# Ten unused TensorE products ahead of the first normed block of each half, at three norms of a decoder step

## What is computed

```python
def rmsnorm(x, g):
    xf = x.astype(F32)
    y = xf * lax.rsqrt(jnp.mean(xf * xf, axis=-1, keepdims=True) + EPS)
    return y.astype(x.dtype) * g
...
        x = x + rmsnorm(o, p['norm_mix_post'][l])
        f, cp = conv_ffn(rmsnorm(x, p['norm_ffn_pre'][l]), p['w_up'][l], p['conv_w'][l],
                         p['conv_b'][l], p['w_down'][l], conv_prev[l])
        new_conv.append(cp)
        x = x + rmsnorm(f, p['norm_ffn_post'][l])
```

## Time and profile before

| | before |
|---|---|
| median of 3 runs | 1521.39 us |
| lowest, highest | 1520.93, 1525.54 us |
| span of the profiled execution, first to last instruction | 1519.0 us |
| what the median has over that span | 2.4 us |
| PE busy, share of the span | 1413.4 us, 93% |
| PEld / DVE / ACT / POOL busy | 86% / 64% / 38% / 42% |
| mean granted TensorE clock | 0.971 of full speed |

### The profile page before, as it was taken

One profiled execution on the slowest core, in us unless ns is written; L12 is line 12 of the kernel. 1 busy time (PEld: TensorE's weight loads), 2 busy tenths in 40 slices (PEclk: granted clock), 3 DMA queues, 4 the chain that ended last, 5 costly groups with the idle time before them and its releaser, 6 DMA issues.

```text
span 1519.0 us, 32537 instructions
## 1 busy us (share of the span) xinstructions
PE 1413.4 (93%) x12097; PEld 1313.9 (86%) x12097; DVE 976.7 (64%) x1658; ACT 576.7 (38%) x1019; POOL 638.5 (42%) x420
## 2 busy tenths in 40 slices
PE   6986978989999999999799989999989999999997
PEld 6984758979999999999699966657889999999997
DVE  5769967576773167765748688753677761376755
ACT  4544354344432133422415235432454431234323
POOL 1586422304444334433177888402223443344430
PEclk9998789989999999999999999999999999999999
DMA  5344364213333232332145769995213233233321
GB/s 173 114 117 79 63 169 123 83 44 85 99 94 98 77 97 83 102 98 75 45 121 164 226 175 308 331 340 157 69 57 97 84 103 90 83 91 88 104 83 62
DMA packets 289082, 180.47 MB, mean 119 GB/s; under 512 B 54248, under 2 KB 274572, under 8 KB 288924
## 3 DMA queue, kind: packets, MB, share of 16 engines
q1 hardware_dynamic: 288412, 179.07, 40.9%
q10 hardware_dynamic: 576, 0.13, 0.0%
HBM read 167.10 MB, written 10.63 MB: 117 GB/s over the span
## 4 chain that ended last, share of the span: by engine, by line
PE 70%; DVE 14%; issue 8%; ACT 2%; SPq 2%; DMA 1%; POOL 1%; DVEq 0%; ACTq 0%; POOLq 0%
PE big L2649 58%; PE big L2715 3%; PE misc L2800 2%; DVE tmp L1261 2%; PE big L2746 2%; DVE y L1738 1%; DVE rstd L1219 1%; DVE x L1744 1%; DVE w_lo L1208 1%; DVE x_lo L1251 1%; SPq L597 1%; PE misc L2770 1%; ACT yc L2506 1%; DVE cp L1261 1%; ACT w_hi L2144 1%
## 5 line engine op out<-in xcount | busy, mean ns | idle before, releaser
L949 POOL TENSOR_TENSOR w_lo<-raw,w_hi 128x1024 fp32r<-128x1024 f32 (+2 forms) x153 | 393.8, 2574 | 708.9 <-ACT w_hi L2144 548.4
L2144 ACT ACTIVATE w_hi<-raw 128x1024 fp32r<-128x1024 f32 (+2 forms) x179 | 198.5, 1109 | 582.1 <-PE big L2649 539.0
L2649 PE MATMUL big<-x_hi,w_hi 128*128 128x264 f32 x1984 | 406.7, 287 | 8.4 <-DVE uc L1827 2.8
L2649 PE MATMUL big<-x_hi,w_lo 128*128 128x264 f32 x1984 | 400.8, 283 | 0.0
L2649 PE MATMUL big<-x_lo,w_hi 128*128 128x264 f32 x1984 | 398.8, 283 | 0.0
L2649 PEld LDWEIGHTS big<-x_hi,w_hi 128*128 128x128 f32 x1984 | 305.9, 189 | 13.1 <-issue 4.7
L2649 PEld LDWEIGHTS big<-x_lo,w_hi 128*128 128x128 f32 x1984 | 305.6, 189 | 0.0
L2649 PEld LDWEIGHTS big<-x_hi,w_lo 128*128 128x128 f32 x1984 | 305.3, 189 | 0.0
L1831 DVE SCALAR_TENSOR_TENSOR yc<-uc,convw,yc 128x512 f32<-128x512 f32 x88 | 136.7, 1554 | 113.2 <-ACT yc L2506 113.2
L2649 PE MATMUL big<-h_hi,w_hi 128*128 128x264 f32 x616 | 125.1, 284 | 6.3 <-DVE h_lo L1846 6.3
L2649 PE MATMUL big<-h_hi,w_lo 128*128 128x264 f32 x616 | 123.9, 282 | 0.0
(11 more groups left out here) (434 smaller groups left out, 2330.8 us busy)
## 6 DMA issues: line engine op xcount, KB each, us to landing
raw<-in_w_up SPq DMA_DIRECT2D x88, 512.0 KB, 3.9
raw<-in_w_down SPq DMA_DIRECT2D x32, 704.0 KB, 4.7
areas<-in_cache_k SPq DMA_DIRECT2D x41, 384.0 KB, 4.5
areas<-in_cache_v SPq DMA_DIRECT2D x41, 384.0 KB, 4.7
raw<-in_w_in SPq DMA_DIRECT2D x16, 512.0 KB, 4.2
raw<-in_w_out SPq DMA_DIRECT2D x16, 512.0 KB, 4.2
raw<-in_w_kv SPq DMA_DIRECT2D x12, 512.0 KB, 4.6
spare<-in_cache_k SPq DMA_DIRECT2D x12, 384.0 KB, 4.5
```

Of the source, the lines that this page charges most:

```text
L949: pool.tensor_tensor(w_lo[slot][:, 0:kb, :], raw[slot][:, 0:kb, :], w_hi[slot][:, 0:kb, :].bitcast(F32), ALU.subtract).then_inc(lo_made, 1)
L2144: A.activation(w_hi[slot][:, 0:kb, :], raw[slot][:, 0:kb, :], ACT.Copy).then_inc(hi_made, 1)
L2649: ins = pe.matmul(big[2 * slot + b_][:, 0:c1 - c0], w[slot][:, k, :], r[:, c0:c1], start=(k == 0 and n_ == 0), stop=(k == kb - 1 and n_ == 2))
```

## The change

Ten products that nothing reads are added twice at each of the three norms. `spin(o, 5)` issues five pairs of 128-column products of `meanw` (as weights) and `ident` (as the moving operand) into PSUM bank o; the real product that follows starts its bank anew and overwrites it. The first ten stand ahead of block k = 0 of half 0 in panel 0, the second ten ahead of block k = 0 of half 1 in panel 0. In half 0 the wait for the PSUM bank moves ahead of the spin, and the wait for w_lo stays behind it.

```diff
+SPUN = (5, 5)
...
+            def spin(o, count):
+
+                for _ in range(count):
+                    for c in range(2):
+                        pe.matmul(o[:, P * c:P * c + P], meanw[:], ident[:], start=True, stop=True)
+
             def first_pair(base, name, before):
 
                 add = x_stats(name)
@@
                         q = base + p_
                         slot = q % 2
                         if b_ == 0:
+                            pe.wait_ge(panel_read, q - 1)
+                            if p_ == 0:
+                                spin(big[2 * slot], SPUN[0])
                             pe.wait_ge(lo_made, q + 1)
-                            pe.wait_ge(panel_read, q - 1)
                         for k in range(KD):
                             if p_ == 0:
+                                if b_ and k == 0:
+                                    spin(big[2 * slot + 1], SPUN[1])
                                 x_split(KD * b_ + k)
```

## The result

Over 13 runs each, the changed kernel took 1531.13 us in the median (1523.25 to 1533.23) and the kernel before 1525.76 us (1520.76 to 1530.24): ratio 1.0035, 95% interval 1.002 to 1.005. That is 5.4 us slower, 3 to 8 by the interval. The sign and the place were as predicted, and the size was close (7.1 us forecast, 1.0047). The kernel before itself spreads over 9.5 us from run to run. The three runs that the prediction started from, which are among the 13, had their median 4.4 us low, and its profiled execution (span 1519.0) was one of the two fastest. Two executions of the kernel before beside the experiments took 7594 and 4704 us, and the ratios leave them out.

What follows compares the result with a forecast made beforehand. PE was taken to set the pace from panel 1 on, DVE at each norm's start. First ten 0, second ten 3 x 2.36 = 7.1 us, clock 0: 1521.4 + 7.1 = 1528.5 us, range 1522.0 to 1532.5.

Steps and rivals of the forecast that it cites:

- The first ten are hidden: Start of half 0, panel 0: ten products take 2.4 us while PE waits for DVE, so they cost 0.
- They save nothing: First gap of each norm: filling it should keep the clock up, but DVE sets the pace there; gain nothing.
- rival 2: At the norms: low-clock stretches thought covered by DVE cost too, all five go, 11.9 us saved, 1516.6 us; chance 0.05.
- The second ten cost in full: Ahead of half 1, panel 0, where PE has no cover: 2.4 us at each norm, 3 x 2.36 = 7.1 us.
- The clock at nothing, kept for the range: Low-clock stretches at the norms may come or go, 1.7 us each, no sign; mean 0, used for the range.
- Rival 1: Through the norms the clock stays at 2.4 GHz, three costly stretches go, 6.1 us saved against 7.1, 1522.4 us; chance 0.13.
- Rival 3: Layer 1 attention: page loads absorb the 4.7 us of f0 and x1, only f1's 2.4 remain, 1523.8 us; chance 0.07.
- Rival 4: Added products: a record costs 0.23 us without load overlap, three times ten 13.8 us, 1535.3 us or more; chance 0.07.

Runs made afterwards that it cites:

- e2: The changed kernel with only the first ten products at each norm, none in the second place; ratio 0.9995 to the kernel before.
- e6: The changed kernel with twenty products in the first place and none in the second; ratio 1.0012 to the kernel before.
- e7: The changed kernel with ten products in the first place, ten ahead of the second w_lo wait, none before half 1; ratio 1.0000 to the kernel before.
- e1: The changed kernel without its products, only the PSUM bank wait moved; ratio 1.0001 to the kernel before.
- e11: The changed kernel without its products, as e1, profiled once more; 1527.45 us.
- e3: The changed kernel with only the second ten products at each norm; ratio 1.0039 to the kernel before, 6.0 us slower.
- e5: The changed kernel with no first products and twenty in the second place; ratio 1.0091 to the kernel before, 13.9 us slower.
- e8: e4 plus six products (f0, f1) or ten (x1) behind the last block of the norm; ratio 0.9982 to the kernel before.
- e9: e8 plus ten products in the first place and eight ahead of block 6 of half 0; ratio 0.9978 to the kernel before.
- e4: The changed kernel with its products replaced by ten at each norm ahead of the second w_lo wait (panel 1, half 0); ratio 0.9986 to the kernel before.

## Why the prediction came out as it did

**The first ten are hidden: right.** The prediction had them stick out 0.4 us at f0, under the wait of block 1. They took 2.2 us and not 2.4, and block 0 was not late at all: it starts 2.02 us behind the end of `last_pair` in both kernels. e2 gave 0.9995.

**They save nothing: right in the sum, half right in the reason.** The prediction said that the low stretches at 314 and 1096 lie under DVE, and they do: ACT took up the post-norm's second root at the same point of its order with the clock up, 8.46 us behind the end of `last_pair` against 8.45 before:

```profile
320.40 0.41 ACT L2481 ACTIVATE y<-x 128x264 f32<-128x264 f32 x1
320.71 0.45 ACT L2178 ACTIVATE sd<-misc,eps 128x256 f32<-128x256 f32 x1
```

That disposes of rival 2. What it missed: in half 0 the pace is DVE's, block 6 starts 12.0 to 12.2 us behind `last_pair` at f0 and f1 in all thirteen profiles, whatever the clock does, and a clock that stays up only leaves idle time ahead of it. The kernel before's trace had this wait too, at x1, where the clock had been up, and the prediction counted only the one behind it (PE in order of time):

```profile
735.39 0.39 PE L2746 MATMUL big<-x_hi,w_hi 128*128 128x264 f32 x1 [2.09 <-DVE x_lo L1251]
```

The clock then fell at a later wait. In all twelve norms with the first gap filled and the one at block 6 open (after, e2, e6, e7) it fell within 6 us of block 6's start, in ten of them within 1.2 us: in the changed kernel at 324.7, 741.1 and 1109.7, with block 6 at 324.27, 735.16 and 1108.61. In the fifteen norms with neither the first gap nor the second filled (before, e1, e11, e3, e5) it fell within 6 us there in nine, and not at f1 of the kernel before.

**The second ten cost in full: right, with the price a little high.** A record took 0.11 us and not 0.118, so ten are 2.2 us and three times ten 6.6 instead of 7.1. e3 measured 6.0 and e5 13.9 us. This is the change's whole loss as far as the runs can tell; the first ten's part lies by e2 between 3 us gained and 1.4 lost. The Trainium skill ("TensorE: Matmul & The Clock Gate", "Back-to-back issue gap") gives a sustained 81 ns for a load and product of 128 columns. The trace doesn't agree for these float32 products, with 0.11 us a record.

**The clock at nothing, kept for the range: right.** The three norm sections sum to 91.6 when no fall costs anything (e8, e9); the three profiles of the kernel before's work (before, e1, e11) stand 3.3 to 4.5 us above that, the changed kernel's 101.55 - 91.6 - 6.6 = 3.3, of which 1.6 at x1 and 1.6 at f1. The price that e3 and the changed kernel paid, (101.55 + 102.81) / 2, less the mean of 95.93, 94.94 and 96.11, is 6.5 us. The sum thus holds, and the forecast 7.1 us lie within the interval of 3 to 8 that the timed runs leave, as 6.6 do.

**Rival 1, the clock held: not by this change.** It needs the later waits filled too. e9 did that, and its 3.4 us are near the 4.0 us that 95.66 - 91.65 allow. So the mechanism of the rival exists, and its place was wrong; the prediction's 6.1 us for it also rested on one profile with much low clock at f0.

**Rival 3, the delay absorbed: no.** e5 lost all that its products cost, across the attention too. **Rival 4, dearer products: no**; the steps are 0.11 us.

**The base was off.** The predicted 1528.5 us was built on 1521.39 us, the median of three runs; thirteen gave 1525.76. The forecast difference added to that would have been 1532.9, against 1531.13 measured, and just above the stated range. The low base and the difference forecast too high (7.1 against 5.4 us) offset each other in part, so that the 1528.5 were only 2.6 us off; that much is luck, and what bears out the mechanism is the difference and the runs that take it apart. Rival 4's 1535.3 should read 1535.2 by its own terms (1521.4 + 13.8); nothing hangs on it.

What stays open: e7 against e4. That e7's first ten harm is seen in one profile each, and the timed ratios don't separate the two. Open too is what decides at which wait the clock falls: the rows say where it fell, and no run here fixes it.

## What to carry to other kernels

Products that only keep TensorE busy are free where another engine sets the pace, as long as they end within its slack, and cost their full steps where TensorE does; the idle bracket in front of the next real product tells which it is. Filling one wait in a stretch that another engine paces doesn't shorten the stretch, and the clock can still fall at the next wait. So look first at the last wait ahead of the stretch that TensorE paces (e4), or fill all of them (e9, where the clock stayed up in the one profile taken); the first alone (e2) gave nothing that could be measured. Before you build on a profiled span, see how far the same work differs from run to run: here the spread was 9.5 us, three times the largest gain.

## What the runs showed of the hardware

- A low clock can be harmless: at f0 of the kernel before, 6.75 us at 1.2 GHz (from 314.35) cost nothing, since the work at half speed filled waits for DVE, and left no wait at block 6, which started 12.02 us behind `last_pair` as in the changed kernel at 2.4 GHz.
- The same work in the attention section took 154.7 to 161.3 us. The stretches of before and of e7 from 920 to 950 us (shortest and longest attention), DMA in GB/s in the last column:

```profile
920.00:950.00 30.00, 28.36 (x295) 18.08 (x289) 24.16 (x39) 17.62 (x49) 26.42 (x16) 1.00 0.96 324
```

```profile
920.00:950.00 30.00, 28.30 (x293) 17.82 (x291) 25.71 (x40) 17.27 (x48) 25.13 (x15) 1.00 0.93 310
```

The page loads ran at 324 GB/s in one and 310 in the other with the same loads. The section's length also goes with the stretches at 1.2 GHz that the rows show inside it, some 3.4 us each: one in the kernel before's profile (154.7 us), two in e2, e8 and e3 (155.3, 157.2 and 158.8), four in e9 and e7 (160.6 and 161.3), and three in the seven others (157.5 to 159.9). Which of the two is the cause wasn't tried.
- A float32 product of 128 columns with 128x128 weights costs 0.11 us a record at 2.4 GHz, two records each: 40 records took 1129.94 - 1125.56 = 4.38 us in e5. Weight load and product overlap; one after the other they would take 0.23 us by the prediction's prices of 0.115 and 0.11.
